# Stick-breaking scores of two heads in one step, alternately in the two row halves of the array

## What is computed

```python
z = jnp.einsum('bqhd,bkhd->bhqk', qb, k_all).astype(f32) * scale
causal = k_pos[None, :] < q_pos[:, None]
log_keep = jnp.where(causal, jax.nn.log_sigmoid(-z), 0.0)
after = lax.cumsum(log_keep, axis=3, reverse=True) - log_keep
w = jnp.where(causal, jnp.exp(jax.nn.log_sigmoid(z) + after), 0.0)
return jnp.einsum('bhqk,bkhd->bqhd', w.astype(v_all.dtype), v_all)
```

## Time and profile before

| | us |
|---|---|
| median of 3 runs | 1167.33 |
| lowest and highest | 1165.99, 1169.71 |
| the profiled execution, device time | 1164.51 |
| its span, first to last instruction | 1162.8 |
| PE busy in it | 1104.1 (95%) |
| DVE, ACT, POOL busy | 806.6, 621.8, 116.0 |
| the attention stage, from the first value rows to the first `x_rows` | 85.14 to 167.58 |

### The profile page before, as it was taken

One profiled execution on the slowest core, in us unless ns is written; L12 is line 12 of the kernel. 1 busy time (PEld: TensorE's weight loads), 2 busy tenths in 40 slices (PEclk: granted clock), 3 DMA queues, 4 the chain that ended last, 5 costly groups with the idle time before them and its releaser, 6 DMA issues.

```text
span 1162.8 us, 18498 instructions
## 1 busy us (share of the span) xinstructions
PE 1104.1 (95%) x7648; PEld 995.8 (86%) x7648; DVE 806.6 (69%) x1014; ACT 621.8 (53%) x817; POOL 116.0 (10%) x147
## 2 busy tenths in 40 slices
PE   6999899999999899899999999999899999999995
PEld 6988779999977899899999999989667778788883
DVE  6315685866788978986436624535589998888884
ACT  6336782434595876532217513321276777778773
POOL 2002330002044000000000000000101000000041
PEclk9999999999999999999999999999799999999999
DMA  9431111233020453534527503102899999999997
GB/s 303 143 116 37 37 41 55 60 105 115 1 56 1 120 140 100 169 109 145 167 79 273 162 1 110 37 1 84 342 337 395 420 409 377 399 395 387 377 279 175
DMA packets 94655, 205.25 MB, mean 177 GB/s; under 512 B 4336, under 2 KB 70040, under 8 KB 81640
## 3 DMA queue, kind: packets, MB, share of 16 engines
q1 hardware_dynamic: 85792, 173.88, 42.3%
q0 software_dynamic: 5584, 19.81, 5.7%
q10 hardware_dynamic: 3192, 10.34, 2.2%
HBM read 182.41 MB, written 21.61 MB: 175 GB/s over the span
## 4 chain that ended last, share of the span: by engine, by line
PE 72%; DVE 11%; ACT 9%; issue 4%; DMA 3%; ACTq 0%; POOL 0%; SPq 0%; POOLq 0%; DVEq 0%
PE ps L2795 35%; PE ps L3140 10%; PE ps L1122 6%; DVE buf_r L1056 5%; ACT buf_r L1049 3%; PE ps L1132 3%; PE ps L3329 2%; PE ps L3345 2%; PE ps L2916 1%; DVE buf_r L1271 1%; ACT buf_r L509 1%; DMA buf<-in_w_gate_e 1%; PE ps L3108 1%; PE ps L3111 1%; PE ps L3104 1%
## 5 line engine op out<-in xcount | busy, mean ns | idle before, releaser
L2795 PE MATMUL ps<-buf_r,buf_r 128*128 128x288 f32 (+1 forms) x3312 | 435.7, 291 | 6.2 <-ACT buf L1823 2.6
L2795 PEld LDWEIGHTS ps<-buf_r,buf_r 128*128 128x128 f32 x3312 | 423.4, 189 | 10.3 <-issue 6.7
L1056 DVE TENSOR_TENSOR buf_r<-buf,buf_r 128x2048 fp32r<-128x2048 f32 x92 | 205.1, 2285 | 0.0
L1122 PE MATMUL ps<-buf_r,buf_r 128*128 128x512 f32 x720 | 174.6, 398 | 0.0
L1049 ACT CAST buf_r<-buf 128x2048 fp32r<-128x2048 f32 x92 | 171.4, 1912 | 0.3 <-DMA buf<-in_w_down_e 0.2
L1122 PEld LDWEIGHTS ps<-buf_r,buf_r 128*128 128x128 f32 x720 | 133.2, 188 | 29.8 <-issue 0.5
L3140 PE MATMUL ps<-buf_r,buf_r 128*128 128x288 f32 x1008 | 138.9, 297 | 9.4 <-ACT buf L2000 4.4
L3140 PEld LDWEIGHTS ps<-buf_r,buf_r 128*128 128x128 f32 x1008 | 135.8, 190 | 11.4 <-issue 9.5
L494 DVE TENSOR_TENSOR buf_r<-buf,buf_r 128x2048 fp32r<-128x2048 f32 (+1 forms) x33 | 74.3, 2255 | 37.6 <-ACT buf_r L488 37.5
L488 ACT CAST buf_r<-buf 128x2048 fp32r<-128x2048 f32 (+1 forms) x37 | 69.8, 1887 | 56.7 <-PE ps L2819 39.7
L1132 PE MATMUL ps<-buf_r,buf_r 128*128 128x512 f32 x384 | 89.8, 389 | 1.0 <-DVE buf_r L1299 1.0
(11 more groups left out here) (378 smaller groups left out, 1460.7 us busy)
## 6 DMA issues: line engine op xcount, KB each, us to landing
buf<-in_w_gate_e SPq DMA_DIRECT2D x32, 1024.0 KB, 8.6
buf<-in_w_up_e SPq DMA_DIRECT2D x32, 1024.0 KB, 7.5
buf<-in_w_down_e SPq DMA_DIRECT2D x32, 1024.0 KB, 7.9
buf<-in_w_in SPq DMA_DIRECT2D x16, 1024.0 KB, 5.9
buf<-in_w_in SPq DMA_DIRECT2D x17, 512.0 KB
buf<-in_w_mem_kv SPq DMA_DIRECT2D x8, 1024.0 KB, 7.2
y_rows<-buf ACTq DMA_DIRECT2D x14, 512.0 KB, 8.7
buf<-in_x_prompt SPq DMA_DIRECT2D x8, 512.0 KB, 5.5
```

Of the source, the lines that this page charges most:

```text
L1056: nc.vector.tensor_tensor(e_lo(t), e_raw(t), e_hi(t), ALU.subtract).then_inc(wl_ready, 1)
L1122: last = nc.tensor.matmul(bank(b), r32(a[:, k, :]), w[:, i, :], start=(k == 0 and j == 0), stop=(k == KD - 1 and j == 2))
L2795: last = nc.tensor.matmul(out, a, b, start=(k == 0 and j == 0), stop=(k == len(parts) - 1 and j == 2))
```

## The change

- For the prompt heads, PE computes the scores of two heads, `u` and `u + 1`, in steps 0, 2, 4 and 6, and none in steps 1, 3, 5 and 7. The products alternate between the lower and the upper half of the array's rows. The odd head's scores go to banks 6 and 7 and the second half of bank 2 (`score_cols`). A new semaphore `third_scored` makes the even head's product into bank 2 wait for the odd head's.
- ACT copies both heads' scores out in the even steps, the odd one's in two pieces.
- The value rows move: after step 1 they are done in steps 3 (two), 5 (two) and 7 (one) and not in 2, 3 and 4, on PE ahead of that step's sums and no longer behind them. They use banks 5, 3, 4, 5, 3, 0, 1, 0, 1, 0.
- At the head of PE's steps 4, 6 and 8, before the scores, stands a wait for ACT's copies of the value rows of the step before (`kv_rows` 17, 19, 20), since they lie in the banks of the scores.
- `values` in steps 4 and 6 waits for the copies of both heads' scores, since it writes bank 6 or 7. `scores(6)` waits for `ysb_out(0)`.
- The transposes of the old keys in step 0 use banks 3 and 4.
- POOL's stores of the value rows move from step 6 to 8, and ACT's rounding of the second weight tile of the next stage (`split_high(W_X + 1)`) from step 6 to 7.

```diff
--- before.py
+++ after.py
@@ -536,9 +536,9 @@
         wo_psum, x1_ready = sem("wo_psum"), sem("x1_ready")
         mkv_psum, mkv_rows, km_psum, km_ready = (sem(n) for n in ("mkv_psum", "mkv_rows", "km_psum", "km_ready"))
         Q_MEM, Q_ROWS = 4, 6
-        (ms_psum, nm_ready, px_ready, rr_ready, pn_ready, pt_psum, pt_ready, ot_psum, ot_ready) = (
+        (ms_psum, nm_ready, px_ready, rr_ready, pn_ready, pt_psum, pt_ready, ot_psum, third_scored) = (
             sem(n) for n in ("ms_psum", "nm_ready", "px_ready", "rr_ready", "pn_ready", "pt_psum", "pt_ready",
-                             "ot_psum", "ot_ready"))
+                             "ot_psum", "third_scored"))
         mo_psum, x2_ready = sem("mo_psum"), sem("x2_ready")
         half_added, two_ready = sem("half_added"), sem("two_ready")
 
@@ -611,9 +611,10 @@
         T_Z = dict(B11=5, B21=6, T2=7, T1=8, T3=9, T4=10, B22=11)
 
         U_ = 10
-        V_FILL = ((0, 1), (2, 3, 4), (5, 6), (7, 8), (9, ))
-        FILL_BANK = 6
-        V_BANK = (6, 7, 3, 4, 5, 6, 7, 6, 7, 6)
+        V_FILL = ((0, 1), (2, 3, 4), (), (5, 6), (), (7, 8), (), (9, ))
+        FILL_BANK = 3
+        V_BANK = (5, 3, 4, 5, 3, 0, 1, 0, 1, 0)
+        V_FREED = (0, 0, 0, 1, 2, 0, 0, 0, 0, 0)
         X_FILL = 2
         STEPS = 4 * NC_
         Q_FIRST = 4
@@ -632,6 +633,13 @@
             if u < SBH:
                 return {0: [(1408, 3, P)], 1: [(1024, 2, 2 * P)], 2: [(896, 1, P)], 3: []}[kc]
             return {0: [(256, 2, P), (1536, 2, P)], 1: [(1536, 2, P)], 2: [(1280, 2, P)], 3: [(1024, 2, P)], 4: []}[kc]
+
+        def score_cols(u, kc):
+
+            o, n = keycols(u, kc)
+            if u < SBH and u % 2:
+                o = 1280 if kc == 2 else 3072 + o
+            return o, n
 
         RAW_STEPS = 4
 
@@ -1687,7 +1695,7 @@
                     pool.wait_ge(mt_stored, 16)
                     pool.wait_ge(sp_raw, RAW_STEPS * u + RAW_STEPS)
                     nc.gpsimd.tensor_copy(r32(LBH[u % 2]), LB[u % 2]).then_inc(lh_ready, 1)
-                if i == 6:
+                if i == 8:
                     rows_out("sb_v", VR, 20)
             pool.wait_ge(ysb_ready, 5)
             pool.wait_ge(out_stored, 16 * KV_STORES)
@@ -1830,7 +1838,11 @@
                     act.wait_ge(out_stored, 16 * 2)
                 if u >= 6:
                     act.wait_ge(pv_psum, 2 * ((u - 6) // 2 + 1))
-                nc.scalar.copy(ZSB[u % 6], ps[:, 0:1280]).then_inc(z_copied, 1)
+                if u < SBH and u % 2:
+                    nc.scalar.copy(ZSB[u % 6][:, 0:1024], bank(6, 2))
+                    nc.scalar.copy(ZSB[u % 6][:, 1024:1280], ps[:, 1280:1536]).then_inc(z_copied, 1)
+                else:
+                    nc.scalar.copy(ZSB[u % 6], ps[:, 0:1280]).then_inc(z_copied, 1)
 
             def softplus_log(u):
                 act.wait_ge(z_masked, u + 1)
@@ -1844,7 +1856,10 @@
                 nc.scalar.activation(lb, lb, ACT.Ln, bias=1.0).then_inc(l_ready, 1)
 
             for i in range(U_ + 3):
-                if i < U_:
+                if i < SBH and i % 2 == 0:
+                    z_copy(i)
+                    z_copy(i + 1)
+                elif SBH <= i < U_:
                     z_copy(i)
                 if i >= 3:
                     act.wait_ge(u_ready, i - 2)
@@ -1857,7 +1872,7 @@
                         kv_out(10 + v, V_BANK[v])
                 if i == 2:
                     split_high(act, W_X)
-                if i == 6:
+                if i == 7:
                     split_high(act, W_X + 1)
                 if i == U_:
                     x_out(0)
@@ -2894,8 +2909,8 @@
             def v_rows(v):
                 if v % 5 == 0:
                     pe.wait_ge(wl_ready, W_V + v // 5 + 1)
-                if v >= 5:
-                    pe.wait_ge(kv_rows, 10 + (1, 2, 6, 7, 8)[v - 5])
+                if V_FREED[v]:
+                    pe.wait_ge(kv_rows, 10 + V_FREED[v])
                 kv(10 + v, V_BANK[v])
 
             pe.wait_ge(kv_rows, 10)
@@ -2909,12 +2924,20 @@
                 else:
                     pe.wait_ge(z_copied, u)
                 if u < SBH:
-                    hp, lo = divmod(u, 2)
-                    r = slice(64 * lo, 64 * lo + 64)
-                    for kc in range(4):
-                        o, n = keycols(u, kc)
-                        last = nc.tensor.matmul(ps[:, o:o + n], KTA[r, hp, kc * P:(kc + 1) * P], QT[r, hp, kc * P:LP],
+                    if u == 6:
+                        pe.wait_ge(ysb_ready, 1)
+                    for lo, kc in ((0, 0), (1, 0), (0, 1), (1, 2), (1, 1), (0, 3), (0, 2), (1, 3)):
+                        if (lo, kc) == (0, 2):
+                            pe.wait_ge(third_scored, u // 2 + 1)
+                        r = slice(64 * lo, 64 * lo + 64)
+                        o, n = score_cols(u + lo, kc)
+                        last = nc.tensor.matmul(ps[:, o:o + n], KTA[r, u // 2, kc * P:(kc + 1) * P], QT[r, u // 2, kc * P:LP],
                                                 start=True, stop=True)
+                        if (lo, kc) == (1, 2):
+                            last.then_inc(third_scored, 1)
+                        if (lo, kc) in ((0, 2), (1, 3)):
+                            last.then_inc(z_psum, 1)
+                    return
                 else:
                     pe.wait_ge(q_ready, Q_ROWS)
                     for kc in range(5):
@@ -2994,8 +3017,14 @@
                 tproj(x_bank(i), W_X + i // 2, (i % 2) * P, HTH, HT).then_inc(xb_psum, 1)
 
             for i in range(U_ + 3):
-                if i < U_:
+                if i in (4, 6, 8):
+                    pe.wait_ge(kv_rows, 15 + min(i - 2, 5))
+                if i < U_ and (i % 2 == 0 or i >= SBH):
                     scores(i)
+                if i in (3, 5, 7):
+                    pe.wait_ge(z_copied, i)
+                    for v in V_FILL[i]:
+                        v_rows(v)
                 if i == 0:
                     pe.wait_ge(past_loaded, 32)
                     for b in range(4, 9):
@@ -3009,12 +3038,12 @@
                     x_rows(i - U_)
                 if 2 <= i < U_ + 2:
                     sums(i - 2)
-                if i < len(V_FILL):
+                if i < 2:
                     for v in V_FILL[i]:
                         v_rows(v)
-                if i == 4:
-                    pe.wait_ge(kv_rows, 20)
                 if i >= 4 and i % 2 == 0:
+                    if i <= 6:
+                        pe.wait_ge(z_copied, i + 2)
                     values(i - 4)
 
             for i in range(3, CONV_C):
```

## The result

The changed kernel takes 1174.38 us in the median of 6 runs (1173.13 to 1175.70), the kernel before 1166.66 us in 6 runs beside it. The ratio is 1.0064 with a 95% interval of 1.0051 to 1.0076: slower by 7.5 us (6.0 to 8.9), where +5.3 us, 1172.6 us, was forecast. (The two medians themselves lie 7.7 us apart.)

The account below looks back on a forecast made before the run. PE was taken to bound the stage's first half, a ring of handoffs its second; -9.4 + 0.6 - 5.8 - 1.6 + 13.8 + 3.0 + 0.5 + 4.2 = +5.3 us gave 1172.6 us, range 1170 to 1175 (chance 0.52).

Parts of the forecast that it names:

- What bounds the stage: Attention stage: bound by PE in its first half and by a ring of handoffs between engines in its second.
- Part 1: Scores: four heads' scores go, -9.4 us; four pairs with overlapping row halves take 2.5 us each, +0.6 us.
- Part 3: Heads of steps 4, 6 and 8: new PE waits for value-row copies, 4.7, 4.7 and 4.4 us, together +13.8.
- Part 4: Before the values of steps 4, 6 and 8: waits of 1.5, 1.5 and 0.5 us for score copies and exponential.
- Part 5: Behind the three long waits: a 1.2 GHz spell each, 1.4 us apiece, +4.2 us; bounds 0 and 3 times 2.2.
- A spell costs 1.6 us: Behind each long wait: full cost of a 1.2 GHz stretch, taken as 1.4 since sums may absorb part.
- Part 6: Moved value-row stores, weight-tile load, ACT's rounding, and odd head's mask and passes: all hidden, no cost in the sum.
- The sum: Whole kernel: all terms together +5.3 us, median from 1167.33 to 1172.6 us.
- The signs: Later profile: waits at about 112.5, 134 and 152 us, lower clock behind each, pairs about 2.5 us, first x_rows about 173.
- The clock holds: Rival, three long waits: the clock does not fall behind them, total about the same; chance 0.18.
- The row halves don't overlap: Rival, score pairs: little or no overlap, up to 4.9 us a pair; chance 0.20, half of it above 1179 us.
- The handoff is shorter than drawn: Rival, three waits: about 2 us each, total -6.7 us, 1160.6 us; chance 0.10, shared with any other gain.

Follow-up runs that it names:

- experiment 1: Changed kernel, but in PE's steps 3, 5 and 7 the sums stand ahead of the value rows: 1164.62 us, ratio 0.9979 to the kernel before.
- experiment 2: Changed kernel, but in steps 3, 5 and 7 ACT copies value rows ahead of the three softplus_log passes: 1162.57 us, ratio 0.9964 to the kernel before.
- experiment 4: Changed kernel with 34 useless matmuls behind the sums of steps 3, 5 and 7, filling the long waits: 1167.75 us, ratio 1.0006 to the kernel before.
- experiment 5: Changed kernel with ACT's value-row copies ahead of its passes in step 3, PE's sums ahead of value rows in steps 5 and 7: 1159.70 us, ratio 0.9933.
- experiment 7: Kernel of experiment 5 with one value row each moved into steps 4 and 6, between sums and values: 1158.54 us, ratio 0.9931 to the kernel before.
- experiment 3: Changed kernel, but each pair's four even-head products stand ahead of the four odd-head ones: 1183.61 us, ratio 1.0144 to the kernel before.

## Why the prediction was right, point by point

- *What bounds the stage.* Right: PE in its first half, handoffs in its second. Experiments 1 and 2 moved only the order of unchanged work and took 10 to 11 us off the stage.
- *Part 1, the pairs.* 2.5 us each were taken, 2.44 and 2.47 measured at full clock. The column halves of the values were the right row to go by. The Trainium skill ("TensorE: Matmul & The Clock Gate", Part 3) says that matmuls in distinct row groups run at once; the trace agrees, with 2.44 us for two heads against 2.35 for one.
- *Part 3, the long waits.* 4.7, 4.7 and 4.4 us were forecast, 4.56, 4.56 and 4.28 measured, with ACT's copy of the value rows as the releaser of all three. The price was taken as the chain of passes behind the sums, and experiments 1 and 2 show that this ring is the cause.
- *Part 4.* 1.5, 1.5 and 0.5 us forecast, 1.49, 1.48 and 0.25 measured. The Trainium skill ("TensorEngine Tiling (Array Packing)", PSUM Bottleneck) says that tiling makes TensorE faster but not the emptying of PSUM. The trace agrees: the pair of 2.47 us at 101.65 is followed by three copies on ACT that take 2.46 us (104.22 to 106.68), where one head's scores of 2.35 us had one copy of 1.13.
- *Part 5, the clock.* The mechanism was right, its size too small: 4.2 us were taken for the three waits, and experiment 4 gives 6.0. The step that failed is "A spell costs 1.6 us", of which "a part of it may fall on the sums of steps 4 and 6". The first wait cost 1.6, but behind the second the whole pair and behind the third the scores and a piece of the sums ran at 1.2 GHz, since the clock had fallen within the wait and came back only 4.5 and 4.8 us after its end, against 3.4 in the first. Nothing of it fell into the waits before the values: they are 1.49 and 1.48 us with it, and 1.49 both without it (experiment 4). The bound of 2.2 us each was the better value.
- *Part 6.* Right in that all is hidden. POOL issues the store at 169.75 (about 165 was forecast) and nothing waits for it; ACT's rounding runs at 161.57 beside the scores of step 8.
- *The sum.* +5.3 forecast, +7.5 measured, of which +5.7 lies in the stage. There the clock term is 1.8 us above the forecast, the waits 0.7 and the pairs 0.2 below it, and 0.4 us of gain have no term. So the stage came out within 0.6 us of the forecast partly because errors of opposite sign cancelled. What lies outside the stage, 1.8 us in the medians, was forecast at nothing and is not settled (the interval is 1.4 us to either side): the profiled spans differ by 2.1 us ahead of it and 1.9 us behind it. In the nine profiles here the first scores start between 78.65 and 80.88 us with the same program ahead of them, and the part behind the stage takes 995.2 to 997.3 us. So both vary by 2 us between kernels that are the same there, and the kernel before had nearly the best of both in its profile.
- *The signs.* The three waits began at 114.2, 137.0 and 157.4 us, where 112.5, 134 and 152 were forecast. The first differs by the 2.1 us ahead of the change alone; the third was drawn some 3 us too early, which the sum doesn't use.
- *The rivals.* "The clock holds" would have been right without the low clock: experiment 4 makes that case and measures a draw (1.0006). "The row halves don't overlap" fell with the first pair. Its ground that every second float32 matmul brings a weight load was misread: the trace has a load for each, 16 loads of 128 columns for the 16 matmuls of a pair, and they don't hold it up (2.44 us). "The handoff is shorter than drawn" is what experiment 1 makes out of the order, with 2.7 us less than the kernel before where the rival's sum has 6.7.

## What to carry to other kernels

When filler work is moved, follow the buffer that it fills to whoever empties it: a copy queued behind passes that wait for PE's own later work turns the filler into a stall, and swapping two neighbours on either engine takes 10 us off again. A saving on the bounding engine counts only with the handoffs redrawn around it; here -9.4 us of matmuls became +7.5, and with two blocks moved -7.7. The three long waits here cost TensorE their own 13.4 us and another 6.0 us in slow matmuls behind them; shorter ones, of about 2 us, cost between nothing and 1.7 us more.

## What the runs showed of the hardware

Equal waits don't bring equal clocks. The wait of 2.13 us at 386.89 in the earlier trace rows left the clock at 1.00, and the 12 matmuls behind it took 1.66 us to the next start:

```profile
388.55 0.29 PE L3159 MATMUL ps<-buf_r,buf_r 128*128 128x288 f32 x1
```

The same wait in the changed kernel was followed by the lower clock:

```profile
394.77 2.84 PE L3169 MATMUL ps<-buf_r,buf_r 128*128 128x288 f32 x12 [2.13 <-ACT buf L2015]
397.41 0.44 PE L3188 MATMUL ps<-buf_r,buf_r 128*128 128x288 f32 x1
```

Nothing near it was changed, and such losses are about 1 us (2.64 against 1.66 here). All nine profiles have this wait at 2.12 or 2.13 us: in the kernel before and in experiment 2 the clock stays at 1.00, in the other seven it falls. Likewise the wait before `sums(2)` is 2.20 us in experiment 5, with slow sums behind it, and 2.19 in experiment 7, with fast ones. So neither the length of such a wait nor the code beside it tells whether the clock falls. What is left is the moment at which the wait comes, but no run moved that alone, so it stays open.

In experiment 3, where a pair uses one half of the array's rows at a time, the clock also stayed down for longer. Behind the second long wait (4.56 us in both kernels) it was 0.50 throughout the pair and the sums, 12 us, where it was back at 0.99 within 4.6 us of the start of the alternating pair in the changed kernel:

```profile
120.00:130.00 10.00, 9.38 (x21) 5.72 (x22) 2.75 (x5) 2.55 (x5) 0.61 (x3) 0.52 0.00 0
...
146.00:158.00 12.00, 11.38 (x29) 7.72 (x30) 2.40 (x5) 4.15 (x7) 2.61 (x6) 0.50 0.00 0
```

```profile
146.00:149.00 3.00, 2.47 (x16) 2.06 (x14) 0.49 (x1) 2.78 (x4) 1.40 (x5) 0.99 0.00 0
```

The first fence is experiment 3, the second the changed kernel; columns as in the earlier trace rows. Whether that comes from the one half in use, or from anything else in which the two kernels differ there, was not tried.
